# Output stage of a streaming encoder layer in two parts, with each tile's normalisation in two VectorE passes

## The reference, cut to what matters

```
x    = layer_norm(alpha * x + mixed @ w_out)                 # ln1_g, ln1_b
s    = sigmoid(x @ w_router);  sel = s + router_bias         # 64 experts in 8 groups
grp  = sum of the best 2 of each group;  keep the best 4 groups
top_e = top 6 of sel within those;  w = s[top_e] / sum * 2.5
routed = sum over k of w[k] * (silu(x@w_gate[e]) * (x@w_up[e])) @ w_down[e]
shared = (silu(x@ws_gate) * (x@ws_up)) @ ws_down             # one expert for all
y    = layer_norm(alpha * x + routed + shared)
```

## Time and profile before

| what | value |
| --- | --- |
| median of 3 runs | 1629.74 us (1627.55 to 1631.99) |
| the profiled execution | 1625.14 us, its span in the trace 1623.4 us |
| busy share: PE, DVE, ACT, POOL | 82%, 67%, 51%, 48% |
| mean clock granted to PE | 0.934 of full |
| moved by DMA | 330.42 MB, 204 GB/s over the span |

### The profile page before, as it was taken

The page is one execution under the profiler, slowest core; times in us unless marked ns, Lnnn a source line. Parts: engine busy times, 40 slices in busy tenths (PEclk is TensorE's granted clock), DMA queues, the critical chain, the costliest instruction groups (busy, mean ns, idle before and its releaser), DMA issues. The chain is left out here.

```text
span 1623.4 us, 22981 instructions
## 1 busy us (share of the span) xinstructions
PE 1325.6 (82%) x6073; PEld 1043.5 (64%) x6073; DVE 1090.9 (67%) x1459; ACT 824.6 (51%) x942; POOL 783.0 (48%) x801
## 2 busy tenths in 40 slices
PE   1396989779669999841999998999999888899930
PEld 1254656566357888731788887888778767678720
DVE  5930454353255777633789997889798777789828
ACT  2311101010452333202688887888688676778835
POOL 2477605320421334432367775677566545467720
PEclk9998989899879999975999999999999999999975
DMA  9323165371551111106699979998999999999647
GB/s 312 133 56 80 32 63 40 67 80 9 97 176 53 64 68 66 65 27 251 250 323 319 312 260 352 355 351 282 328 319 316 335 329 336 336 344 324 219 118 295
DMA packets 113056, 330.42 MB, mean 204 GB/s; under 512 B 30656, under 2 KB 61376, under 8 KB 88432
## 3 DMA queue, kind: packets, MB, share of 16 engines
q1 hardware_dynamic: 79136, 264.84, 48.7%
q0 software_dynamic: 27344, 63.16, 14.8%
q10 hardware_dynamic: 6528, 1.84, 0.7%
HBM read 287.06 MB, written 68.91 MB: 219 GB/s over the span
## 5 line engine op out<-in xcount | busy, mean ns | idle before, releaser
L1889 DVE TENSOR_TENSOR moe_up_l<-rt_raw_up,moe_up_h 128x2048 fp32r<-128x2048 f32 x154 | 353.2, 2295 | 114.3 <-ACT moe_up_h L1706 114.0
L1706 ACT ACTIVATE moe_up_h<-rt_raw_up 128x2048 fp32r x154 | 294.1, 1912 | 133.0 <-DMA rt_raw_up<-in_w_up_dram 101.6
L1797 POOL DMA_INDIRECT acc<-moe_y,moe_idx_s x77 | 238.7, 3100 | 65.5 <-POOL moe_idx_s L1794 46.0
L1829 PE MATMUL moe_p_gu<-moe_up_h,moe_x_h 128*128 128x512 f32 x616 | 244.8, 397 | 6.7 <-DVE moe_up_l L1889 4.7
L1829 PE MATMUL moe_p_gu<-moe_up_h,moe_x_l 128*128 128x512 f32 x616 | 244.3, 397 | 0.0
L1829 PE MATMUL moe_p_gu<-moe_up_l,moe_x_h 128*128 128x512 f32 x616 | 244.0, 396 | 0.0
L685 PE MATMUL mix_proj<-co_hT,co_win 128*128 128x384 f32 (+1 forms) x768 | 238.1, 472 | 6.5 <-PEq L103 6.5
L685 PEld LDWEIGHTS mix_proj<-co_hT,co_win 128*128 128x128 f32 x768 | 146.4, 192 | 94.6 <-issue 9.0
L1794 POOL COPY moe_idx_s<-rt_idx 128x1 int32 (+1 forms) x77 | 111.9, 1454 | 166.7 <-ACT moe_y L1729 166.7
L1910 DVE TENSOR_TENSOR moe_dn_l<-rt_raw_dn,moe_dn_h 128x2048 fp32r<-128x2048 f32 x77 | 175.9, 2284 | 6.7 <-ACT moe_dn_h L1752 6.7
L1841 PE MATMUL moe_p_dn<-moe_dn_h,moe_hid_h 128*128 128x512 f32 x308 | 130.7, 424 | 46.1 <-DVE moe_dn_l L1910 44.6
(11 more groups left out here) (405 smaller groups left out, 2290.5 us busy)
## 6 DMA issues: line engine op xcount, KB each, us to landing
rt_raw_up<-in_w_gate_dram SPq DMA_DIRECT2D x64, 1024.0 KB, 9.3
rt_raw_up<-in_w_up_dram SPq DMA_DIRECT2D x64, 1024.0 KB, 13.3
rt_raw_dn<-in_w_down_dram SPq DMA_DIRECT2D x64, 1024.0 KB, 7.2
final_x<-acc SPq DMA_DIRECT2D x18, 512.0 KB, 13.2
co_win<-in_w_in_dram SPq DMA_DIRECT2D x16, 512.0 KB, 5.0
acc<-trunk_blank SPq DMA_DIRECT2D x9, 512.0 KB, 9.4
resid<-trunk_x SPq DMA_DIRECT2D x9, 512.0 KB, 2.6
proj_res<-resid SPq DMA_DIRECT2D x9, 512.0 KB, 3.2
```

The lines of the kernel that those rows point to most:

```text
L1706: act.activation(up_h[:, par, half, :, :], raw_up[:, bass.ds(slot, 1), half, :, :].rearrange("p a k n -> p (a k) n"), ACT.Copy).then_inc(u ...
L1797: pool.indirect_dma_start(out=io.acc[par], in_=y[:, par, :], in_offset=None, out_offset=bass.IndirectOffsetOnAxis(ap=idx_s[:, par:par + 1] ...
L1829: mm = pe.matmul(p_gu[:, par, :].rearrange("p (a n) -> p a n", a=2), x, w, start=(i == 0), stop=(i == len(terms) - 1))
L1889: low = tt(up_l[:, par, half, :, :], raw_up[:, bass.ds(slot, 1), half, :, :].rearrange("p a k n -> p (a k) n"), up_h[:, par, half, :, :].b ...
```

## The change

Six things are done together.

1. `project_stage` is cut in two parts. Part 1 goes over the 9 tiles with the output projection, the normalisation and the router alone; on PE it is `project(i, 0)`, `route(i-2)`, `project(i, 1)`, `turn_x(i-1)`. The router is now 8 plain f32 matmuls of 64 columns on the transposed tile, which ACT keeps in the place of `gT` and `ycT` (`turned`). Part 2 goes over the tiles with the shared expert: `up(j)`, ranks of tiles in pairs, `down(j-1)`, `turn_hid(j)`; DVE does the placing there.
2. The normalisation is, on DVE, one pass `(x - mean) * gain` and one pass `* rstd + bias`, both 1024 columns. ACT gives the standard deviation and the negative mean. POOL has no part in it.
3. The stores of `tok` and `acc` are issued by SP. `acc[1]` starts as `alpha * x` (ACT, `scaled`) and `acc[0]` as the shared expert's output (ACT, `shared`), instead of zero and their sum; the trunk's nine stores of zeros are gone.
4. `routing_stage` is gone as a stage: its DVE work, its gather of the lists and its transposes stand in part 2, and the prefetch of the first three experts' weights on SP follows the projection.
5. At the start of `expert_stage`, ACT and DVE split the weights of the first two blocks ahead of their tokens, and DVE instead of POOL clears `xg`.
6. `gate_stage` has no piece for the router's weights any more, and its last two steps take one piece each. Silu takes the place of a sigmoid and a product.

The core of the diff:

```diff
-        PIECES = [("out", k) for k in range(KD)] + [("rt", 0)] + [("in", k) for k in range(KD // 2)] + [("dn", 0), ("dn", 1)]
+        PIECES = [("out", k) for k in range(KD)] + [("in", k) for k in range(KD // 2)] + [("dn", 0), ("dn", 1)]
         AFTER = [range(0), range(0, 1), range(1, 2), range(2, 4), range(4, 5), range(5, 7), range(7, 8), range(8, 10),
-                 range(10, 11), range(11, 12), range(12, 13), range(13, 15)]
-        DVE_PIECES = KD + 3
+                 range(10, 11), range(11, 12), range(12, 13), range(13, 14)]
+        DVE_PIECES = KD + 2
 
...
             for i in range(1, N_TILES):
                 sp.wait_ge(s_z, 2 * i)
                 sp.dma_start(res[:, :], io.resid[i * P:(i + 1) * P, :]).then_inc(s_res, 16)
+                finished(i - 1)
+            sp.sem_inc(rt.up_in[1], 32)
+            sp.sem_inc(rt.down_in[1], 16)
+            sp.wait_ge(s_po, 2 * N_TILES)
+            for e in range(DN_SLOTS):
+                prefetch(e)
+            finished(LAST)
+            for j in range(N_TILES):
+                store(j)
+                if j == 1:
+                    prefetch(DN_SLOTS)
+            for k in range(2):
+                sp.wait_ge(s_tok[k], 16 * len(range(k, N_TILES, 2)))
+            sp.wait_ge(s_acc, 16 * 2 * N_TILES)
 
...
-            pool.wait_ge(s_ln, 32)
-            for i in steps:
-                if i < N_TILES:
-                    pool.wait_ge(s_gain, i + 1)
-                    pool.tensor_tensor(x[:, i % 3, :], x[:, i % 3, :], lnb[:, :], ALU.add).then_inc(s_x, 1)
-                    pool.wait_ge(s_x, i + 1)
-                    pool.dma_start(io.tok[i * P:(i + 1) * P, :], x[:, i % 3, :]).then_inc(s_tok[i % 3], 16)
-                if i >= 2:
-                    j = i - 2
-                    pool.wait_ge(s_ao, 2 * j + 2)
-                    pool.dma_start(io.acc[0][j * P:(j + 1) * P, :], x[:, j % 3, :]).then_inc(s_acc[j % 3], 16)
-                    put(j)
-            for k in range(2):
-                pool.wait_ge(s_put[k], 16 * TOP_K * len(range(k, N_TILES, 2)))
-            for k in range(3):
-                pool.wait_ge(s_tok[k], 16 * len(range(k, N_TILES, 3)))
-                pool.wait_ge(s_acc[k], 16 * len(range(k, N_TILES, 3)))
+            for i in range(N_TILES):
+                pool.wait_ge(s_dst, i + 1)
+                for k in range(TOP_K):
+                    pool.indirect_dma_start(out=io.slots, in_=pay[:, i, k, :], in_offset=None,
+                                            out_offset=bass.IndirectOffsetOnAxis(ap=dst[:, i, k:k + 1], axis=0),
+                                            bounds_check=bound, oob_is_err=False).then_inc(s_put, 16)
+            pool.wait_ge(s_at, 1)
+            pool.wait_ge(s_put, 16 * TOP_K * N_TILES)
+            pool.indirect_dma_start(out=lists.rearrange("p s w -> p (s w)"), out_offset=None,
+                                    in_=io.slots.rearrange("(r s) w -> r (s w)", s=P),
+                                    in_offset=bass.IndirectOffsetOnAxis(ap=at[:, 0:1], axis=0)).then_inc(s_lists, 16)
+            pool.wait_ge(s_lists, 16)
 
         @block.tensor
...
+            def route(i):
+                pe.wait_ge(s_xt, 2 * i + 2)
                 if i:
-                    pe.wait_ge(s_hl, i)
+                    pe.wait_ge(s_lg, i)
+                else:
+                    pe.wait_ge(s_wr, 16)
+                for k in range(KD):
+                    src = (gT, ycT)[k // KH]
+                    mm = pe.matmul(pm[:, 0:NE], src[:, k % KH, i * P:(i + 1) * P], w_rt[:, k, :], start=(k == 0),
+                                   stop=(k == KD - 1))
...
-                    rank(i - 2)
-                if i < N_TILES:
-                    project(i, 1)
-                if i >= 2:
-                    down(i - 2)
-                if i == N_TILES + 1:
+            up(0)
+            rank(0)
+            route(LAST - 1)
+            turn_hid(0)
+            up(1)
+            turn_x(LAST)
+            down(0)
+            route(LAST)
+            turn_hid(1)
+            for j in range(2, N_TILES):
+                up(j)
+                if j == 4:
                     count()
-                if 1 <= i <= N_TILES:
-                    enter(i - 1)
+                if 1 <= j - 2 < PAIRS:
+                    rank(j - 2)
+                if j == LAST:
+                    turn_tables()
+                down(j - 1)
+                turn_hid(j)
+            down(LAST)
+            turn_lists()
 
         @block.vector
...
             def norm(i):
-                link(v.bn_aggr(mv[:, :], stats[:, :, :]), s_zd)
                 v.wait_ge(s_std, i + 1)
+                v.wait_ge(s_neg, i + 1)
                 link(v.reciprocal(rs[:, 0:1], rs[:, 0:1]))
-                link(stt(out=rs[:, 1:2], in0=mv[:, 0:1], scalar=-1.0, in1=rs[:, 0:1], op0=ALU.mult, op1=ALU.mult),
-                     s_rstd)
-                v.wait_ge(s_nm, i + 1)
                 if i == 0:
                     v.wait_ge(s_ln, 32)
-                tt(x[:, i % 3, :], x[:, i % 3, :], lng[:, :], ALU.mult).then_inc(s_gain, 1)
-
...
+                link(stt(out=x[:, i % 2, :], in0=x[:, i % 2, :], scalar=rs[:, 1:2], in1=lng[:, :], op0=ALU.add,
+                         op1=ALU.mult))
+                stt(out=x[:, i % 2, :], in0=x[:, i % 2, :], scalar=rs[:, 0:1], in1=lnb[:, :], op0=ALU.mult,
+                    op1=ALU.add).then_inc(s_x, 1)
...
+            in_low(0)
+            for i in range(N_TILES):
+                if i:
+                    total(i - 1, 1)
+                if i >= 3:
+                    choose_experts(i - 3)
+                if i:
+                    norm(i - 1)
+                total(i, 0)
+                in_low(i + 1)
...
+            total(LAST, 1)
+            choose_experts(LAST - 2)
+            in_low(LAST + 2)
+            norm(LAST)
+            hidden(0)
+
+            hid_low(0)
+            take_ranks(0)
+            choose_groups(LAST - 1)
+            in_low(LAST + 3)
+            choose_experts(LAST - 1)
+            hidden(1)
+
+            hid_low(1)
+            in_low(LAST + 4)
+            place(0)
+            choose_groups(LAST)
+            hidden(2)
+
+            hid_low(2)
+            in_low(LAST + 5)
+            choose_experts(LAST)
+            place(1)
+            hidden(3)
+
+            for n in (1, 2, 3):
+                j = n + 2
+                hid_low(j)
+                in_low(LAST + 3 + j)
+                take_ranks(n)
+                for i in pair(n):
+                    place(i)
+                hidden(j + 1)
+
+            hid_low(LAST - 2)
+            in_low(LAST + 1 + LAST)
...
                 if isinstance(n, int) and n == 0:
                     for k in range(2):
+                        up_high(k, k, up_high_first(k, k), 1)
                         x_high(k, k)
-                        up_high(k, k, up_high_first(k, k), 1)
...
                 if isinstance(n, int) and n == 0:
                     for k in range(2):
+                        up_low(k, k)
                         x_low(k, k)
-                        up_low(k, k)
```

More of the change, by code:

```diff
@@ L1134, in project_stage @@
[L1134 to L1142 removed]
+        s_ln, s_v, s_pool = m.sem("ln"), m.sem("vch"), m.sem("poolch")
+        s_res, s_alpha, s_ax, s_acc = (m.sem(n) for n in ("res", "alpha", "ax", "acc"))
@@ new lines, in count, with up @@
+            def count():
+                pe.wait_ge(s_mask, N_TILES)
+                pe.wait_ge(s_xt, 2 * N_TILES)
+                for j in range(N_TILES):
+                    mm = pe.matmul(pt[:, 0, 0:NE], ones_b[:, :], mask_b[:, j, :], start=(j == 0),
+                                   stop=(j == N_TILES - 1))
+                mm.then_inc(s_count, 1)
+            def up(j):
+                q = N_TILES + j
+                pe.wait_ge(s_inl, q + 1)
+                if j < 2:
+                    pe.wait_ge(s_z, 2 * LAST + 1)
+                else:
+                    pe.wait_ge(s_hid, j - 1)
+                split_product(po[:, 0, j % 2, :], (in_h[:, q % 2, :, :], in_l[:, q % 2, :, :]), (w.in_h, w.in_l),
+                              slice(0, 2 * D_EXP)).then_inc(s_up, 1)
@@ new lines, in turn_tables, with turn_lists @@
+            def turn_tables():
+                pe.wait_ge(s_eo, 1)
+                for k, col in enumerate((in0, in1, third, odd)):
+                    tr = pe.transpose(pt[0:1, 0, k * P:(k + 1) * P], col[:, 0:1], keep.ident[:, :])
+                tr.then_inc(s_t, 1)
+            def turn_lists():
+                pe.wait_ge(s_lists, 16)
+                for k in range(2):
+                    tr = pe.transpose(pt[:, 1, k * P:(k + 1) * P], lists[:, :, k], keep.ident[:, :])
+                tr.then_inc(s_turned, 1)
@@ new lines, in _ @@
+            choose_experts(LAST)
[6 more added lines that the diff above has]
+                take_ranks(n)
+                for i in pair(n):
+                    place(i)
+                hidden(j + 1)
```

(6 more changed lines are left out.)

643 lines of the change are left out of this document (303 added, 340 removed).

## The result

The changed kernel takes 1619.34 us (median of 5 runs, 1617.77 to 1620.84) against 1628.98 for the kernel before (5 runs beside it): ratio 0.9943 [0.9925, 0.9960]. That is faster by 9.6 us where 43.7 were forecast, and above the top of the range (1608).

A forecast was written before the change was run, and what follows sets the result against it. PE was taken to bound the project and expert stages, with a wait between. Gains of 2.0 + 35.7 + 6 = 43.7 us took the profiled 1625.1 to 1581.5; the median lies 4.6 above: 1586 us, range 1568 to 1608.

The forecast's parts named there:

- Part 2: Project stage, second part: PE's last product at P0+213, puts from P0+147 to P0+221, 5 us for DVE holding POOL.
- P0: Time of the first project matmul, 480.52 in the trace before; forecast to move to 478.5.
- S: Start of the expert stage, P0+268.2 before; forecast P0+232.5, with the earlier P0 37.7 us earlier.
- First put and pitch: Puts in part 2: the first at P0+147, 54 in one row 1.27 us apart, the last issued at P0+221.
- From the gather to S: From the lists' gather at P0+223.5, through POOL's drain of 8.2 us and a barrier, to S at P0+232.5.
- Start of the expert stage: From S to the first expert matmul: 14 us instead of 20.2, a gain of 6 us (4 to 8).
- Gate stage: End of the gate stage: one of POOL's two low parts moves a step earlier, a gain of 2.0 us.
- the tie: Part 1, per tile: PE at 13.5 us and DVE at 13.5 set the round together, taken as 13.6.
- stretched round: Rival in part 1: slower f32 router or PE-DVE gaps add 1.5 us a round; gain 30, 1600 us; chance 0.14.
- the residual's loop: Rival in part 1: the single buffer's residual load delays rounds, 1653 us at a landing of 13; slower, chance 0.06.
- costed at nothing: Expert stage: every later block shifts as a whole with the earlier start, at no cost.
- puts held by DVE: Rival in part 2: DVE's work holds puts to 3.4 us apart; gain 13, 1617 us; chance 0.11.

The follow-up runs named there:

- rests: Changed kernel with POOL waiting for the landing of each tile's six puts before the next six; 1615.16 us, ratio 0.9915.
- spread one: Changed kernel with landing waits, block 0 multiplied before block 1 is turned, and tiles 0 to 3 ranked and placed in part 1; 1584.26 us, ratio 0.9709.

## Why the prediction was wrong, by its steps

**The step that failed** is in "Part 2": PE's own end at P0+213, and "That isn't what ends the stage". The own work was sized rightly (216 without puts beside it, 217.5 with rests). But I had let 54 puts in one row lie beside it and priced only what others do to the puts (5 us for DVE's hold). What the row does to the others was in no term: 41 us (257.4 against 216). In three more profiles with the same order of puts the last product comes at 248.1, 251.7 and 255.4, so the hold costs 32 to 41. In the terms of the sum the profile gives 0.8 + 5.1 + 0.7 = 6.6 us for the forecast 2.0 + 35.7 + 6; nearly all that is missing is in S. In the kernel before, the puts come six a tile between other work of POOL and so never make such a row; the trace of before did not show the cost, but I took the new row for free without naming that.

**First put and pitch.** 152.3 for 147: five late. The pitch inside a row is 1.28, nearly as said, but POOL also waited 5.10 for the second tile's placing and 8.12 for the fifth's, and the last put came at 234.4 for 221. The first of these waits is DVE's own order: that placing ends at P0+164.9, and at 164.2 without puts beside it. The second is the row's doing: 196.1 against 180.2.

**From the gather to S.** The 9.0 forecast is right where the puts end last: with the rests the lists' gather is issued at P0+240.8, POOL's drain ends last, 7.6 after it, and S is at 249.9, 9.1 after the gather. In the changed kernel and in the spread one PE's product comes last, and S is 5.7 behind it.

**Start of the expert stage**, the second step that failed. 14 forecast, 19.5 measured, so 0.7 us for the 6. The mechanism was right for block 0, whose transposes end at S+9.9. I had overlooked that PE's order turns block 1 as well before it multiplies block 0, and that block 1's gather is the one held beside DVE's weight split: its index copy took 1.91 and its issue 2.25 where 0.18 and 1.05 are usual. With the order mended it is 12.1, two less than said.

**Gate stage.** 58.1 us before and 57.3 after, from its first instruction to P0: 0.8 for the 2.0. In this profile P0 lies 4.7 earlier; the rest of that comes from the mixing stage, which the change does not touch. It took 333.1 us here, 338.7 before and 333.7 to 342.0 in the other eleven profiles, so that is scatter.

**Right:** part 1 (121 forecast, 121.2 measured), though by PE alone: DVE was busy 96 of 121 us, so the tie that I saw was none, and neither the stretched round nor the residual's loop came. The two passes took 1.285 us each and a round 13.86 for 13.6; the last total started at P0+121.7.

**The expert stage**, costed at nothing. Among the changed kernels it passes an earlier start on: in the spread kernel's profile the first expert matmul is 38.3 us earlier than in the changed kernel's and the execution 35.3 shorter. Against before it is less clear. From the first expert matmul to the last expert product it is 794.8 us in before's only profile, 801.1 in the changed kernel's, and 797.9 to 805.1 in the seven other changed ones with no stream added. The profiled execution is therefore only 4.3 us shorter than before's (1620.84 against 1625.14), while the medians differ by 9.6. Whether the change makes that stage longer stays open.

**The rivals.** The time, 1619, is nearly that of "puts held by DVE" (1617), but that is luck, for its mechanism did not come: the median put took 0.972 us and the longest 1.40. It is the other way about, the puts hold DVE, PE and ACT. The Trainium skill's figure of some 3100 ns for a GpSimd transfer beside a VectorE copy ("SBUF — State Buffer", section "A bandwidth-pool intuition that's wrong (but worth ruling out)") does not show in any put here: the longest of all versions took 1.69 us. The page measured it beside a copy, and no put here lay beside a long one, so this doesn't test the figure itself.

With both failed steps mended, by rests and by the other order, the time is 1610 us and not the forecast, since the rests put S at 250.7 for 232.5. Only with 24 puts moved into part 1 does it come to 1584. That this is near the forecast of 1586 doesn't confirm the sum: that kernel places its puts elsewhere, and its S (227.9) and start (11.9) are other than forecast.

## What to carry to other kernels

When a change gathers many small indirect stores in one place, ask not only who delays them but whom they delay: count how many come in a row, at which pitch, and which engines must exchange signals meanwhile. Here a landing wait after six (pitch 1.6) took the hold away but made the row itself end later, and spreading the puts over an earlier, PE-bound part (24 of them for some 1.5 us) was worth far more. Where an order puts two blocks' preparation ahead of the first product, the later block's transfer is on the path.

## What the runs showed of the hardware

An unbroken row of indirect stores issued by GpSimd at 1.28 us each (1.15 with 16 rows) holds the other engines from some 10 to 25 us into the row on, with DMA at 0.02: linked DVE operations go from one in 0.24 us to one in about 1.1, PE's matmuls without any wait to one in 1.4 or 2.8, and answers come up to 48 us late. DVE is held without PE's stream beside it, and 16 rows a store are enough; plain stores at twice the rate don't do it; at 1.44 us it is nearly gone, at 1.79 gone; and it is over some microseconds after the row.

Open is which path carries the backlog. All executions here are recorded ones (each has its span and granted clock), so it could also be the path of the records; if so, a run without them would show no hold. The Trainium skill, "NOTIFIC — the notification-queue block", section "7.1 Overflow: three behaviours, one of which stalls the engine", says that this block's internal pipeline always applies back pressure rather than lose a record inside the block, and that a count of its stalls other than zero would mean that it had throttled an engine. No run here shows that it did, and a run without records wasn't tried.
